# Two unsplit products instead of five in the first pair of four stages, and X's parts in another order

## The chip, the cores and the metric

The kernel runs on one core of a Trainium2 chip. The metric is the device time of one execution in microseconds (us). The engines are TensorE (PE in the profile; PEld is its weight load), VectorE (DVE), ScalarE (ACT), GpSimd (POOL) and SyncE (SP), which issues most of the DMAs.

## The reference

One layer of a streaming encoder, for 1024 prompt frames and 32 sample frames (T = 1056 tokens, D_MODEL = 1024, D_FF = 2816), all in float32:

```
attn_branch = o.reshape(B, T, Q_W) @ w_attn_out
lru_branch = (h * jax.nn.gelu(yg)) @ w_lru_out
x = x + (g_a * attn_branch + g_b * lru_branch) @ w_o
gate, up = jnp.split(rms_norm(x, ffn_norm) @ w_gate_up, 2, axis=-1)
x = x + (jax.nn.silu(gate) * up) @ w_down
```

Ahead of it stand the input projection, windowed attention and a gated linear recurrence. The change touches the products with `w_attn_out` and `w_down` alone.

## The kernel before

The last five matrix products run from about 728 us to the end. They are cut into seven stages (`PHASES`): W_lru_out, W_attn_out, W_o, W_gate_up, and W_down in three stages of 8, 8 and 6 tiles of its 22 input tiles (`DOWN_ROWS` = 4, 4, 3 for each half). A stage goes over *pairs*: a pair is two tiles of 128 output features for all 1056 tokens. There are 4 pairs in a stage and 22 in W_gate_up, 46 in all, numbered through.

**Seven products.** A pair computes a 2 x 2 block product (output tile x token half, with the contraction cut in two halves) with seven block products instead of eight. This needs sums of W's quarters (`w_sum`, GpSimd, four for each pair, into `wsum` and in place into `praw`) and of X's quarters (`x_sum`, VectorE, four for each stage, in place in `acc` and `spare`). X's seven parts are the same for all pairs of a stage; part 2 is X's second sum, part 5 a plain quarter. A product is done for two token quarters of 264, each with 4 chunks of 128 of the contraction (3 in the last stage), into the banks of `BANKS`: products 4, 5 and 6 add onto the banks of 0, 1 and 3 once those are copied or combined.

**Split and unsplit.** Most products are split: each operand is a high part rounded to the fast matmul format (fp32r) and a low part, its remainder, and a chunk is three matmuls (high x high, low x high, high x low of X and W). The high parts are made by ScalarE (`w_high` L1153 into `wsh`, `x_high` L1170 into `xh`), the low parts of W by GpSimd (`w_low` L549 into `wsl`), those of X by VectorE (`part_low` L1518 into `xl`). W's parts go through a ring of four slots (`SLOTS`): the high part of a split product waits until TensorE has ended the split product four before it. X's parts stay for the whole stage. A product in `FP32` is unsplit in the first pair of its stage: TensorE takes float32 operands as they are, one matmul for a chunk (two records in the trace), and waits for the raw part only. This bridges the time until X's parts are made.

**Combination.** VectorE adds the products up (`combine`): `first_sums` (L1615, L1619) after product 2, then one combination for each of products 3 to 6. In the W_down stages (`combine_added`) three adds of 528 columns (L1675) put the sums onto the rows of the residual right behind `first_sums`; in W_attn_out (`combine_gated`) gates are applied behind each product.

**Order.** Each engine's order is written out by hand. VectorE's is the loop over pairs that the change edits. `LOWS` and `HIGHS` say in which order X's parts are counted, for the waits; `x_high_after` and `w_high_after` say behind which product ScalarE makes a part; GpSimd goes product by product (`w_sum`, `w_low`). A sum of W that overwrites `wsum` waits until its last reader is done: GpSimd's own `w_low` for a split product, TensorE for an unsplit one.

Of the kernel before, what the change touches and what calls it, by code (L numbers as in the profile page):

```python
# [155 lines left out]
PLAIN_BANKS = {(0, 0): 2, (1, 1): 0, (0, 1): 4, (1, 0): 6}  # L156
FP32 = ((0, 1, 2, 3, 4, 5, 6), (2, 3, 4, 5, 6), (2, 3, 4, 5, 6), (0, 2, 3, 4, 5, 6)) + ((2, 3, 4, 5, 6),) * 3
X_FIRST = tuple(f + (f == PLAIN) for f in PHASE_FIRST[:PHASES])
BANKS = ((0, 1), (4, 5), (2, 3), (6, 7), (0, 1), (4, 5), (6, 7))
LOWS = ((0, 1, 2, 3, 4, 5, 6),) * 3 + ((1, 0, 2, 3, 4, 5, 6),) + ((0, 1, 2, 3, 4, 5, 6),) * 3  # L160
HIGHS = ((0, 1, 2, 4, 5, 3, 6), (0, 1, 4, 5, 2, 3, 6), (0, 1, 2, 5, 4, 3, 6), (1, 0, 5, 2, 3, 4, 6)) + ((0, 1, 4, 5, 2, 3, 6),) * 3
MERGED_LRU = 3 * PAIRS[LRU_OUT]
# [83 lines left out]
def x_high_after():  # L246

    at = {(0, 0): [(LRU_OUT, 2)], (0, 1): [(LRU_OUT, 4), (LRU_OUT, 5)], (0, 2): [(LRU_OUT, 3)], (0, 4): [(LRU_OUT, 6)]}
    for t in range(1, PHASES):
        f = X_FIRST[t]  # L250
        if t == GATE_UP:
            order = {(f, 0): (5, 2), (f, 1): (3,), (f, 2): (4,), (f, 4): (6,)}
        elif t == OUT:
            order = {(f - 1, 0): (0,), (f - 1, 1): (1,), (f, 0): (2, 5), (f, 1): (4, 3), (f, 4): (6,)}
        else:
            order = {(f - 1, 0): (0,), (f - 1, 1): (1,), (f - 1, 4): (4,), (f - 1, 5): (5,),
                     (f, 0): (2,), (f, 1): (3,), (f, 4): (6,)}
        for pr, ks in order.items():
            at.setdefault(pr, []).extend((t, k) for k in ks)
# [7 lines left out]
def build(nc, small_in, x_in, cs_in, w_in, kc_in, vc_in, y_out, kp_out, vp_out, ks_out, vs_out, tail_out):  # L267
# [17 lines left out]
    with ctx:  # L285
# [987 lines left out]
        def _(dve):  # L1273
# [456 lines left out]
            for p in range(N_PAIRS):  # L1730
# [16 lines left out]
                elif first:  # L1747
                    part_low(t, 2)
                elif second:
                    part_low(t, 6 if t in (ATTN_OUT, OUT) else 5)  # L1750
                combine(p, 2)
                if nxt:
                    part_low(nxt, 1)
                if first:
                    if t == LRU_OUT:
                        part_low(t, 2)
                    x_sum(t, 3)
                elif second and t not in (ATTN_OUT, OUT):
                    part_low(t, 6)
# [5 lines left out]
                combine(p, 4)  # L1765
                if first and t in (ATTN_OUT, OUT):
                    part_low(t, 4)
# [3 lines left out]
                elif nxt:  # L1771
                    x_sum(nxt, 2)
                if first:
                    part_low(t, 5 if t in (ATTN_OUT, OUT) else 4)
                combine(p, 6)
# [325 lines left out]
```

## Time and profile before

| | |
|---|---|
| median of three runs | 1692.95 us (1692.91 to 1693.06) |
| the profiled execution | 1695.31 us, its span 1693.5 us |
| TensorE busy | 1638.5 us, 97% of the span |
| VectorE busy | 1063.5 us, 63% |
| GpSimd busy | 965.3 us, 57% |
| ScalarE busy | 619.1 us, 37% |
| matmuls split (xh, xl) | 3 x 2170 records, 1859.5 us of overlapping durations |
| matmuls unsplit (acc, spare with praw, wsum) | 716 records |

Times in a timeline row are microseconds from the span's start, then the length. Matmuls overlap in the records, so the distance between starts tells the pace, not the duration of one. A bracket at the end of a row is the engine's idle time before it and what ended it.

### The profile page before, as it was taken

Reading aid. Unit: us, or ns where it says so; the run is one execution under the profiler, and the core shown is the slowest. Engines: PE = TensorE matmul, PEld = TensorE weight load, DVE = VectorE, ACT = ScalarE, POOL = GpSimd, SP = SyncE. Lnnn points to the kernel's source line nnn. Section 1 sums busy time; section 2 is a strip of 40 time slices with the busy share of each in tenths; the row PEclk is TensorE's granted clock in tenths of the full one; section 3 lists DMA queues with packets and bytes.
Section 4 is the critical chain, followed back from the end, with each engine's and each line's share of the span. In section 5 each row is a group of like instructions: output and inputs, shape, how many; then the busy total and the mean of one; then the engine's idle time right before and its main releaser. Section 6 shows DMA issues by size and latency. Waiting matters only on the chain. (4 is left out here: it accounts for less than half of the span.)

```text
span 1693.5 us, 29231 instructions
## 1 busy us (share of the span) xinstructions
PE 1638.5 (97%) x11306; PEld 1548.2 (91%) x11306; DVE 1063.5 (63%) x1640; ACT 619.1 (37%) x1303; POOL 965.3 (57%) x687
## 2 busy tenths in 40 slices
PE   7999999999999999999899899999999999999999
PEld 4899989988889898898898889999999999998998
DVE  7777774963856556677889678333333334869685
ACT  4354533233342434433334334333333333433242
POOL 4656552321312222287785716877777777786876
PEclk9999999999999999999999999999999999999999
DMA  4111112233113131345541512222243222373734
GB/s 166 50 51 62 62 56 100 67 78 113 53 56 102 56 107 64 103 155 201 178 153 51 194 62 76 101 76 76 76 159 108 76 76 76 137 263 114 257 141 147
DMA packets 72764, 182.12 MB, mean 108 GB/s; under 512 B 14704, under 2 KB 26416, under 8 KB 72000
## 3 DMA queue, kind: packets, MB, share of 16 engines
q1 hardware_dynamic: 51376, 159.13, 26.8%
q10 hardware_dynamic: 21264, 21.27, 4.2%
q8 instruction: 85, 1.39, 0.3%
q14 instruction: 39, 0.32, 0.1%
HBM read 131.36 MB, written 49.28 MB: 107 GB/s over the span
## 5 line engine op out<-in xcount | busy, mean ns | idle before, releaser
L573 PE MATMUL bank<-xh,wsh 128*128 128x264 f32 x2170 | 622.9, 287 | 22.4 <-POOL wsl L549 6.7
L573 PE MATMUL bank<-xh,wsl 128*128 128x264 f32 x2170 | 618.6, 285 | 0.0
L573 PE MATMUL bank<-xl,wsh 128*128 128x264 f32 x2170 | 618.0, 285 | 0.0
L573 PEld LDWEIGHTS bank<-xh,wsh 128*128 128x128 f32 x2170 | 410.4, 189 | 26.1 <-issue 18.1
L573 PEld LDWEIGHTS bank<-xl,wsh 128*128 128x128 f32 x2170 | 410.6, 189 | 0.3
L573 PEld LDWEIGHTS bank<-xh,wsl 128*128 128x128 f32 x2170 | 410.5, 189 | 0.0
L573 PE MATMUL bank<-acth,wh 128*128 128x352 f32 x984 | 329.3, 335 | 4.7 <-POOL actl L511 3.8
L573 PE MATMUL bank<-acth,wl 128*128 128x352 f32 x984 | 319.9, 325 | 0.0
L573 PE MATMUL bank<-actl,wh 128*128 128x352 f32 x984 | 318.6, 324 | 0.0
L499 POOL TENSOR_SCALAR wh<-wraw 128x512 fp32r<-128x512 f32 x104 | 86.0, 827 | 382.4 <-PE bank L573 371.9
L549 POOL TENSOR_TENSOR wsl<-praw,wsh 128x512 fp32r<-128x512 f32 (+1 forms) x157 | 243.8, 1553 | 84.1 <-ACT wsh L1153 83.9
L549 POOL TENSOR_TENSOR wsl<-wsum,wsh 128x512 fp32r<-128x512 f32 (+1 forms) x120 | 187.9, 1566 | 81.6 <-ACT wsh L1153 81.5
L573 PEld LDWEIGHTS bank<-acth,wh 128*128 128x128 f32 x984 | 185.3, 188 | 9.1 <-issue 5.2
L1153 ACT ACTIVATE wsh<-praw 128x512 fp32r<-128x512 f32 (+1 forms) x157 | 96.9, 621 | 255.0 <-PE bank L573 230.2
L573 PEld LDWEIGHTS bank<-actl,wh 128*128 128x128 f32 x984 | 186.0, 189 | 3.3
L573 PEld LDWEIGHTS bank<-acth,wl 128*128 128x128 f32 x984 | 185.3, 188 | 0.4
L501 POOL TENSOR_TENSOR wl<-wraw,wh 128x512 fp32r<-128x512 f32 x104 | 152.2, 1464 | 15.2 <-POOL wh L499 0.2
L1711 DVE TENSOR_TENSOR ev<-bank,ev 128x264 f32<-128x264 f32 x126 | 53.8, 431 | 158.9 <-PE bank L573 158.9
L1153 ACT ACTIVATE wsh<-wsum 128x512 fp32r<-128x512 f32 (+1 forms) x120 | 74.2, 618 | 198.7 <-POOL wsum L545 116.6
L1518 DVE TENSOR_TENSOR xl<-acc,xh 128x2112 fp32r<-128x2112 f32 (+1 forms) x47 | 129.7, 2759 | 22.7 <-ACT xh L1170 22.7
L1615 DVE SCALAR_TENSOR_TENSOR ev<-bank,ev 128x264 f32<-128x264 f32 x90 | 38.6, 429 | 136.4 <-PE bank L573 135.8
L545 POOL TENSOR_TENSOR wsum<-praw,wsum 128x512 f32<-128x512 f32 (+1 forms) x45 | 71.5, 1589 | 80.0 <-PE bank L573 80.0
(170 smaller groups left out, 2394.8 us busy)
## 6 DMA issues: line engine op xcount, KB each, us to landing
praw<-in_weights SPq DMA_DIRECT2D x34, 1024.0 KB, 4.9
wraw<-in_weights SPq DMA_DIRECT2D x52, 512.0 KB, 3.3
h_scratch<-ev SPq DMA_DIRECT2D x44, 264.0 KB, 2.1
acc<-h_scratch SPq DMA_DIRECT2D x4, 2112.0 KB, 12.3
ev<-x_scratch SPq DMA_DIRECT2D x6, 1056.0 KB, 5.0
spare<-x_scratch SPq DMA_DIRECT2D x6, 1056.0 KB, 5.1
praw<-in_weights SPq DMA_DIRECT2D x8, 768.0 KB, 4.7
ta_scratch<-tg ACTq DMA_DIRECT2D x24, 176.0 KB, 1.9
```

What stands on the lines that cost most here:

```text
L499: nc.gpsimd.tensor_scalar(wh[:, u, c], wraw[:, u, c], 1.0, 0.0, ALU.mult, ALU.add).then_inc(split_done, 1)
L501: nc.gpsimd.tensor_tensor(wl[:, u, c], wraw[:, u, c], wh[:, u, c].bitcast(f32), ALU.subtract)\
L545: nc.gpsimd.tensor_tensor(dst, a, b, op).then_inc(wsum_done, 1)
L549: nc.gpsimd.tensor_tensor(w_slot(wsl, p, r), w_part(p, r), w_slot(wsh, p, r).bitcast(f32), ALU.subtract)\
L573: return nc.tensor.matmul(*args, **kw)
L1153: f(w_slot(wsh, p, r), w_part(p, r), ACT.Copy).then_inc(whi_done, 1)
L1518: V.tensor_tensor(xl[k][:, 0:n, :], x_part(t, k), xh[k][:, 0:n, :].bitcast(f32), ALU.subtract)\
L1615: stt(u2(par, n), bank[BANKS[2][n]][:, 0:QB], scale, u2(par, n), ALU.mult, ALU.add).then_inc(u2_done, 1)
L1711: V.tensor_tensor(dst, bank[BANKS[r][n]][:, 0:QB], (u4(par, n), None, u2(par, n), u2(par, n))[r - 3], ALU.add).then_inc(done, 1)
```

## The change

In W_attn_out and the three W_down stages `FP32` holds products 3 and 6 alone, so products 2, 4 and 5 of the first pair are split too. Their X parts move ahead of part 3: `HIGHS` and `LOWS` of these stages become 0, 1, 2, 4, 5, 3, 6. ScalarE makes high 2, 4 and 5 in the last pair of the stage before (where 4 and 5 stood, with 2 ahead), and VectorE makes low 4 and low 5 before products 3 and 4 are combined. With three products more split, each of these stages has three more high and three more low parts of W.

```diff
--- before.py
+++ after.py
@@ -154,11 +154,12 @@
 PLAIN = PHASE_FIRST[GATE_UP]
 PLAIN_ORDER = ((0, 0, 0), (0, 0, 1), (0, 1, 1), (0, 1, 0), (1, 0, 1), (1, 1, 1), (1, 0, 0), (1, 1, 0))
 PLAIN_BANKS = {(0, 0): 2, (1, 1): 0, (0, 1): 4, (1, 0): 6}
-FP32 = ((0, 1, 2, 3, 4, 5, 6), (2, 3, 4, 5, 6), (2, 3, 4, 5, 6), (0, 2, 3, 4, 5, 6)) + ((2, 3, 4, 5, 6),) * 3
+FP32 = ((0, 1, 2, 3, 4, 5, 6), (3, 6), (2, 3, 4, 5, 6), (0, 2, 3, 4, 5, 6)) + ((3, 6),) * 3
 X_FIRST = tuple(f + (f == PLAIN) for f in PHASE_FIRST[:PHASES])
 BANKS = ((0, 1), (4, 5), (2, 3), (6, 7), (0, 1), (4, 5), (6, 7))
-LOWS = ((0, 1, 2, 3, 4, 5, 6),) * 3 + ((1, 0, 2, 3, 4, 5, 6),) + ((0, 1, 2, 3, 4, 5, 6),) * 3
-HIGHS = ((0, 1, 2, 4, 5, 3, 6), (0, 1, 4, 5, 2, 3, 6), (0, 1, 2, 5, 4, 3, 6), (1, 0, 5, 2, 3, 4, 6)) + ((0, 1, 4, 5, 2, 3, 6),) * 3
+LOADED_EARLY = (ATTN_OUT, DOWN, DOWN + 1, DOWN + 2)
+LOWS = ((0, 1, 2, 3, 4, 5, 6), (0, 1, 2, 4, 5, 3, 6), (0, 1, 2, 3, 4, 5, 6), (1, 0, 2, 3, 4, 5, 6)) + ((0, 1, 2, 4, 5, 3, 6),) * 3
+HIGHS = ((0, 1, 2, 4, 5, 3, 6), (0, 1, 2, 4, 5, 3, 6), (0, 1, 2, 5, 4, 3, 6), (1, 0, 5, 2, 3, 4, 6)) + ((0, 1, 2, 4, 5, 3, 6),) * 3
 MERGED_LRU = 3 * PAIRS[LRU_OUT]
 X_LOADED = {ATTN_OUT: 32, DOWN: 64, DOWN + 1: 96, DOWN + 2: 128}
 
@@ -253,8 +254,8 @@
         elif t == OUT:
             order = {(f - 1, 0): (0,), (f - 1, 1): (1,), (f, 0): (2, 5), (f, 1): (4, 3), (f, 4): (6,)}
         else:
-            order = {(f - 1, 0): (0,), (f - 1, 1): (1,), (f - 1, 4): (4,), (f - 1, 5): (5,),
-                     (f, 0): (2,), (f, 1): (3,), (f, 4): (6,)}
+            order = {(f - 1, 0): (0,), (f - 1, 1): (1,), (f - 1, 4): (2,), (f - 1, 5): (4,), (f - 1, 6): (5,),
+                     (f, 1): (3,), (f, 4): (6,)}
         for pr, ks in order.items():
             at.setdefault(pr, []).extend((t, k) for k in ks)
     return at
@@ -1746,8 +1747,10 @@
                     part_low(t, 1)
                 elif first:
                     part_low(t, 2)
+                    if t in LOADED_EARLY:
+                        part_low(t, 4)
                 elif second:
-                    part_low(t, 6 if t in (ATTN_OUT, OUT) else 5)
+                    part_low(t, 5 if t in (LRU_OUT, GATE_UP) else 6)
                 combine(p, 2)
                 if nxt:
                     part_low(nxt, 1)
@@ -1755,7 +1758,9 @@
                     if t == LRU_OUT:
                         part_low(t, 2)
                     x_sum(t, 3)
-                elif second and t not in (ATTN_OUT, OUT):
+                    if t in LOADED_EARLY:
+                        part_low(t, 5)
+                elif second and t in (LRU_OUT, GATE_UP):
                     part_low(t, 6)
                 combine(p, 3)
                 if nxt and nxt != OUT:
@@ -1763,15 +1768,15 @@
                 if first:
                     part_low(t, 3)
                 combine(p, 4)
-                if first and t in (ATTN_OUT, OUT):
+                if first and t == OUT:
                     part_low(t, 4)
                 combine(p, 5)
                 if nxt == OUT:
                     x_sum(nxt, 1)
                 elif nxt:
                     x_sum(nxt, 2)
-                if first:
-                    part_low(t, 5 if t in (ATTN_OUT, OUT) else 4)
+                if first and t not in LOADED_EARLY:
+                    part_low(t, 5 if t == OUT else 4)
                 combine(p, 6)
                 if nxt == OUT:
                     x_sum(nxt, 2)
```

The file grows by one line above the engines' code, so line L1518 of before is L1519 of after, and so on.

VectorE, first pair of the second W_down stage (pair 38), from low 2 on, before (`xl2`, `xl5` are X's low parts, L1552 X's last sum, L1687 a combination):

```order
L1518 TENSOR_TENSOR xl2<-acc,xh2 128x2112 [waits x_part_high]
L1615 SCALAR_TENSOR_TENSOR ev<-bank2,ev 128x264 [waits first_product_copied,product_done]
L1619 SCALAR_TENSOR_TENSOR ev<-bank4,ev 128x264 [waits residual_added,u2_done]
L1615 SCALAR_TENSOR_TENSOR ev<-bank3,ev 128x264 [waits first_product_copied,product_done]
L1619 SCALAR_TENSOR_TENSOR ev<-bank5,ev 128x264 [waits residual_added,u2_done]
L1675 TENSOR_TENSOR ev<-ev 128x528 [waits u4_done,rows_loaded0]
L1675 TENSOR_TENSOR ev<-ev 128x528 x2
L1552 TENSOR_TENSOR acc<-acc 128x4x528 [waits x_part_low,product_done,x_sums,hidden_loaded]
L1687 SCALAR_TENSOR_TENSOR ev<-bank6,ev 128x264 [waits residual_added,product_done]
```

and after the change:

```order
L1519 TENSOR_TENSOR xl2<-acc,xh2 128x2112 [waits x_part_high]
L1519 TENSOR_TENSOR xl4<-acc,xh4 128x2112 [waits x_part_high]
L1616 SCALAR_TENSOR_TENSOR ev<-bank2,ev 128x264 [waits first_product_copied,product_done]
L1620 SCALAR_TENSOR_TENSOR ev<-bank4,ev 128x264 [waits residual_added,u2_done]
L1616 SCALAR_TENSOR_TENSOR ev<-bank3,ev 128x264 [waits first_product_copied,product_done]
L1620 SCALAR_TENSOR_TENSOR ev<-bank5,ev 128x264 [waits residual_added,u2_done]
L1676 TENSOR_TENSOR ev<-ev 128x528 [waits u4_done,rows_loaded0]
L1676 TENSOR_TENSOR ev<-ev 128x528 x2
L1553 TENSOR_TENSOR acc<-acc 128x4x528 [waits x_part_low,x_sums,hidden_loaded]
L1519 TENSOR_TENSOR xl5<-acc,xh5 128x2112 [waits x_part_high]
L1688 SCALAR_TENSOR_TENSOR ev<-bank6,ev 128x264 [waits residual_added,product_done]
```

Low 4 has moved ahead of the first sums, low 5 ahead of the combination of product 3; before, low 4 stood four products on and low 5 in the next pair. X's last sum no longer waits for TensorE's product 2.

ScalarE, from behind product 4 of pair 37 into pair 38, before:

```order
L1153 ACTIVATE wsh0<-wsum 128x512 [waits weight_sums,product_done]
L1170 ACTIVATE xh4<-acc 128x2112 [waits product_done,hidden_loaded]
L1153 ACTIVATE wsh1<-praw1 128x512 [waits pair_weights_loaded1,product_done]
L1170 ACTIVATE xh5<-acc 128x2112 [waits product_done,hidden_loaded]
L1209 ACTIVATE ev<-bank0 128x264 [waits product_done]
L1209 ACTIVATE ev<-bank1 128x264 [waits product_done]
L1170 ACTIVATE xh2<-acc 128x2112 [waits product_done,x_sums]
```

and after (`wsh` is a high part of W, L1209 and L1210 the copy of product 0):

```order
L1171 ACTIVATE xh2<-acc 128x2112 [waits product_done,x_sums]
L1154 ACTIVATE wsh3<-wsum 128x512 [waits weight_sums,product_done]
L1171 ACTIVATE xh4<-acc 128x2112 [waits product_done,hidden_loaded]
L1154 ACTIVATE wsh0<-praw0 128x512 [waits pair_weights_loaded0,product_done]
L1171 ACTIVATE xh5<-acc 128x2112 [waits product_done,hidden_loaded]
L1210 ACTIVATE ev<-bank0 128x264 [waits product_done]
L1210 ACTIVATE ev<-bank1 128x264 [waits product_done]
L1154 ACTIVATE wsh1<-wsum 128x512 [waits weight_sums,product_done]
```

High 2, which waits for X's sums, has moved from behind the copy to the front, with the high parts of W for products 2 and 4 of pair 38 and the copy behind it.

GpSimd, pair 38 from the low part for product 1 on, before:

```order
L549 TENSOR_TENSOR wsl0<-wsum,wsh0 128x512 [waits weight_high]
L545 TENSOR_TENSOR praw0<-praw0 128x4x128 [waits weight_sums]
L545 TENSOR_TENSOR wsum<-praw0,wsum 128x512 [waits product_done]
L545 TENSOR_TENSOR wsum<-praw1 128x512 [waits pair_weights_loaded1]
L549 TENSOR_TENSOR wsl1<-praw1,wsh1 128x512 [waits weight_high]
L549 TENSOR_TENSOR wsl2<-wsum,wsh2 128x512 [waits weight_high]
L545 TENSOR_TENSOR wsum<-wsum,praw1 128x512 [waits product_done,weight_sums]
```

and after, from the same low part on:

```order
L550 TENSOR_TENSOR wsl2<-wsum,wsh2 128x512 [waits weight_high]
L546 TENSOR_TENSOR praw0<-praw0 128x4x128 [waits weight_sums]
L550 TENSOR_TENSOR wsl3<-wsum,wsh3 128x512 [waits weight_high]
L546 TENSOR_TENSOR wsum<-praw0,wsum 128x512 [waits weight_low]
L550 TENSOR_TENSOR wsl0<-praw0,wsh0 128x512 [waits weight_high]
L550 TENSOR_TENSOR wsl1<-wsum,wsh1 128x512 [waits weight_high]
L546 TENSOR_TENSOR wsum<-praw1 128x512 [waits pair_weights_loaded1]
```

Low parts of W for products 2, 4 and 5 have come in, and the sum for product 5 waits for GpSimd's own low part (`weight_low`) where it waited for TensorE (`product_done`).

## Rows read from the trace of the kernel before

**Rows 1.** The page: its span and its first part.
```profile
span 1693.5 us, 29231 instructions
...
PE 1638.5 (97%) x11306; PEld 1548.2 (91%) x11306; DVE 1063.5 (63%) x1640; ACT 619.1 (37%) x1303; POOL 965.3 (57%) x687
```

**Rows 2.** Timeline of TensorE: start, us, group, shapes, count.
```profile
1545.28 3.72 PE L573 MATMUL bank<-acc,wsum 128*128 128x264 f32 x16
1548.84 7.28 PE L573 MATMUL bank<-acc,praw 128*128 128x264 f32 x32
...
1559.52 3.72 PE L573 MATMUL bank<-acc,praw 128*128 128x264 f32 x16
```

**Rows 3.** Windows: stretch, its us, TensorE busy, clock, DMA.
```profile
1496.67:1517.12 20.45, 20.45 (x170) 1.00 0.82 307
1659.76:1675.07 15.31, 15.31 (x128) 1.00 0.39 142
```

**Rows 4.** Timeline of VectorE, second W_down stage.
```profile
1536.12 2.75 DVE L1552 TENSOR_TENSOR acc<-acc 128x2112 f32<-128x2112 f32 x1
...
1542.42 0.76 DVE L1687 SCALAR_TENSOR_TENSOR spare<-bank,spare 128x264 f32<-128x264 f32 x2
1544.84 2.36 DVE L1518 TENSOR_TENSOR xl<-acc,xh 128x2112 fp32r<-128x2112 f32 x1 [1.66 <-ACT xh L1170]
1547.26 0.43 DVE L1615 SCALAR_TENSOR_TENSOR ev<-bank,ev 128x264 f32<-128x264 f32 x1
...
1550.04 4.27 DVE L1675 TENSOR_TENSOR ev<-ev 128x528 f32<-128x528 f32 x3
1554.23 3.42 DVE L1552 TENSOR_TENSOR acc<-acc 128x2112 f32<-128x2112 f32 x1
```

**Rows 5.** Timeline of ScalarE, the same stage.
```profile
1532.28 1.96 ACT L1170 ACTIVATE xh<-acc 128x2112 fp32r<-128x2112 f32 x1
```

**Rows 6.** Timeline of GpSimd, the same stage; in brackets the idle before.
```profile
1536.62 3.40 POOL L545 TENSOR_TENSOR praw<-praw 128x512 f32<-128x512 f32 x1
1549.08 1.27 POOL L545 TENSOR_TENSOR wsum<-praw,wsum 128x512 f32<-128x512 f32 x1 [9.07 <-PE bank L573]
```

**Rows 7.** Waits of TensorE in second pairs (us, times, longest), and two timeline rows.
```profile
PE bank L573 <- DVE ev L1648: 2.2, 2, 1.5
PE bank L573 <- POOL wsl L549: 2.1, 1, 2.1
...
1581.28 0.37 PE L573 MATMUL bank<-xh,wsh 128*128 128x264 f32 x1 [0.54 <-DVE spare L1687]
...
1657.32 0.36 PE L573 MATMUL bank<-xh,wsh 128*128 128x264 f32 x1 [1.03 <-DVE spare L1687]
```

**Rows 8.** Timelines of VectorE and TensorE, first W_down stage.
```profile
1453.20 1.78 DVE L1719 TENSOR_TENSOR ev<-ev 128x528 f32<-128x528 f32 x1
...
1457.50 3.72 PE L573 MATMUL bank<-acc,wsum 128*128 128x264 f32 x16
...
1471.74 3.72 PE L573 MATMUL bank<-acc,praw 128*128 128x264 f32 x16
```

**Rows 9.** Timelines of VectorE and TensorE, third W_down stage.
```profile
1627.18 0.76 DVE L1687 SCALAR_TENSOR_TENSOR spare<-bank,spare 128x264 f32<-128x264 f32 x2
...
1640.23 2.83 PE L573 MATMUL bank<-acc,praw 128*128 128x264 f32 x12
...
1654.21 2.62 DVE L1518 TENSOR_TENSOR xl<-acc,xh 128x1584 fp32r<-128x1584 f32 x1
```

**Rows 10.** Timelines of VectorE and TensorE, W_attn_out stage.
```profile
803.83 3.72 PE L573 MATMUL bank<-acc,wsum 128*128 128x264 f32 x16
...
804.46 0.71 DVE L1654 SCALAR_TENSOR_TENSOR spare<-spare,ev 128x528 f32<-128x528 f32 x1
807.82 3.31 DVE L1518 TENSOR_TENSOR xl<-acc,xh 128x2112 fp32r<-128x2112 f32 x1 [2.65 <-ACT xh L1170]
...
818.07 3.72 PE L573 MATMUL bank<-acc,praw 128*128 128x264 f32 x16
```

## The prediction

> **What bounds the kernel now.** I read the page's busy shares first: TensorE works 97% of the span [rows 1], so the time moves only with what TensorE issues and with what makes it wait. Then I read TensorE's timeline in the stages that change. In the first pair of the second W_down stage products 2 to 6 are unsplit: product 2 is 16 records from 1545.28, product 3 begins at 1548.84, product 6 at 1559.52 [rows 2]. So one unsplit product takes 1548.84 - 1545.28 = 3.56 us, and five of them end at 1559.52 + 3.72 = 1563.24 with no gap. A pair with all seven products split takes 20.45 us, 2.92 us each; with three chunks 15.31, 2.19 each [rows 3]. An unsplit product of three chunks takes 3/4 of 3.56, 2.67 us. A split product is therefore 0.64 us (0.48) shorter, if its parts are ready. The rest of the reading is who makes them ready: VectorE's timeline beside it (all of X's sums and low parts), ScalarE's (the high parts) and GpSimd's (sums and low parts of W).
>
> **What the change removes on TensorE.** In four stages products 2, 4 and 5 of the first pair become split: 3 x 3 x 0.64 + 3 x 0.48 = 5.8 + 1.4 = 7.2 us less matmul time. That is 0.4% of the span, and would be the whole story if no part came late.
>
> **What it adds elsewhere.** Twelve more high parts of W on ScalarE and low parts on GpSimd. ScalarE has room. What matters is VectorE. X's low parts are not new, all seven were made before; but now TensorE needs low 2, 4 and 5 within the first pair, while before it took the raw part there. The order shows VectorE doing low 2, low 4, the two first sums of product 2 (four instructions), three adds of residual rows, X's last sum, and only then low 5. From the end of product 2 TensorE has product 3 (3.56) and product 4 (2.92), 6.48 us, before it wants low 5.
>
> **The chain in the second W_down stage.** VectorE ends the pair before at 1542.42 + 0.76 = 1543.18 [rows 4]. High 2 now stands one pair earlier on ScalarE and waits there for X's second sum, which ends at 1536.12 + 2.75 = 1538.87; with 1.96 us for it [rows 5] it is there by 1540.9, before VectorE is free, and high 4, another 1.96 with one short weight part between, well before low 2 ends. So VectorE goes straight on. What a low part costs depends on GpSimd. With GpSimd idle, low 2 took 2.36 us; the sum beside a busy GpSimd took 3.42, and the three adds 4.27 [rows 4]; GpSimd's own row beside VectorE took 3.40 [rows 6]. I price an X operation at 3.4 where GpSimd has work. It has: the idle of 9.07 us before its row at 1549.08, waiting for the unsplit product 2 [rows 6], is gone with that wait, and three more low parts stand there. Low 2 starts as GpSimd has only begun, so 2.36 + 0.4: 1545.9. TensorE, ready at 1545.28, loses 0.6 and ends product 2 at 1545.9 + 2.92 = 1548.8. Low 4 ends at 1549.3; the sums, 4 x 0.43, at 1551.0; the adds at 1555.3; X's last sum at 1558.7; low 5 at 1562.1. TensorE wanted it at 1548.8 + 6.48 = 1555.3: it **waits 6.8 us**. Product 5 and the unsplit product 6 follow, 2.92 + 3.56 = 6.48, and the pair ends at 1568.6 instead of 1563.24: +5.35. In the next pair TensorE had waited 0.54 us for VectorE [rows 7]; with VectorE's low parts now done earlier that wait goes. Net **+4.8**. Product 6 needs the bank that the combination behind low 5 frees (0.76 us), during product 5: nothing.
>
> **The first W_down stage**, the same way: VectorE is free at 1453.20 + 1.78 = 1454.98 [rows 8]. Low 2 to 1457.9; the low part of W for product 2 stands behind it on GpSimd and takes 1.2 more, so product 2 runs 1459.1 to 1462.0 (before, it began at 1457.50 [rows 8]). The second half of its sums ends at 1463.1, then 4.27 + 3.4 + 3.4: low 5 at 1474.2, pair end 1480.7 against 1471.74 + 3.72 = 1475.46: +5.2, less about 0.5 as above: **+4.7**.
> **The third**, with three chunks: free at 1627.18 + 0.76 = 1627.94; a low part takes 2.62 beside GpSimd [rows 9], and 3/4 of 2.36, 1.8, alone. Low 2 to 1630.0, low 4 to 1632.6, sums 1634.3, adds 1638.6, sum 1641.2, low 5 1643.8; then 2.19 + 2.67 gives 1648.7 against 1640.23 + 2.83 = 1643.06: +5.6, less the 1.03 of the next pair [rows 7]: **+4.6**.
> **W_attn_out** differs: product 2's combination has no three adds. VectorE is free at 804.46 + 0.71 = 805.17 [rows 10] with GpSimd's backlog ahead of it: low 2 at 808.5, so product 2, which began at 803.83 [rows 10], starts 4.7 later and ends at 811.4. Low 4 811.9, sums 813.6, sum 817.0, low 5 820.4 against 817.9 wanted; the end is 820.4 + 6.48 = 826.9 against 818.07 + 3.72 = 821.8, +5.1. But in its second pair TensorE had waited 2.2 us on VectorE's lag and 2.1 on a late low part of W [rows 7], which came of GpSimd waiting for the unsplit product 5. VectorE starts 2.6 us earlier than its row at 807.82 [rows 10], which had waited for high 2, and GpSimd no longer waits: -4.3. Net **+0.8**.
>
> **The sum.** 4.8 + 4.7 + 4.6 + 0.8 = +14.9 us on the profiled span of 1693.5, in which the 7.2 us saved are already counted. That execution took 1695.31 with what lies around the span; the median of the three runs is 1692.95. I add to the median: 1707.9, say **1708.0** (+0.9%).
>
> **The lock.** The rows show that a VectorE operation on two SBUF tensors grows from 2.36 to 3.4 us beside GpSimd, while its operations from PSUM stay at 0.43 [rows 4]. The Trainium skill, "SBUF — State Buffer", section "Who interferes with whom", says that the two engines share a port pair as an exclusive lock: a VectorE instruction with two SBUF inputs and a GpSimd one that reads SBUF block each other for the whole of the first. The trace agrees in kind. By that rule alone each X operation could wait for a full GpSimd one; an estimate from the page's rule, 2.36 + GpSimd's 1.27 = 3.6 us, would be 0.2 us more for each, 3 us more in all. A simple sharing of bandwidth would leave short waits shorter, so the rule speaks against this change.
>
> **Bounds of what the trace does not show.** VectorE unhindered: in a W_down stage low 5 comes 2 x 0.43 (sums of the last half) + 3 x 0.71 (as a 528-column row of [rows 10]) + 2 x 2.36 = 7.7 us after product 2's end, 1.2 after it is wanted. Then a stage gives 3 x -0.64 + 1.2 - 0.5 = -1.2. In W_attn_out low 2 is there at 807.5 and low 5 in time: +1.6 - 4.3 = -2.7. From above: each X operation with the full 3.4 and each low part of W for product 2 another 1.2 late, +1.2 a stage, and nothing regained in W_attn_out's second pair: +8.
>
> **Rivals.**
> *The parts come in time* (the other side). Wait at most 1.2 us: -2.7 - 3 x 1.2 = -6.3, or 1686.6; with no wait at all it would be -7.2, and -4.3, -0.5, -0.5 and -1.0 in the second pairs, 1679.5. A W_down stage wins when low 5 comes less than 6.48 + 1.92 + 0.5 = 8.9 us after product 2's end. For it: GpSimd leaves gaps where ScalarE is held back by its slots. Against: even unhindered VectorE is late, and it has eleven units of GpSimd work beside it.
> *Half hindered.* GpSimd idles during X's last sum and low 5, so 2.36 each: low 5 is 2.1 us earlier, +2.7 a stage; with -1 in W_attn_out, 3 x 2.7 - 0.2 = +7.9: 1701.
> *A second wait.* Putting high 2 ahead on ScalarE, where it waits for X's sum until 1538.87, holds back the W high parts and the copy of product 0 behind it; if the W parts then come late as well, or W_attn_out's second pair regains nothing: 1708 + 4 to 8, 1712 to 1716.
>
> **How the numbers follow.** The forecast 0.62; half hindered 0.15; second wait 0.11; parts in time 0.12. The range 1697 to 1713 holds the forecast and its neighbours and leaves out the last case and the far end of the second wait. Within 0.2% (3.4 us) is about what a measurement of this kernel cannot tell from no change. Faster 0.12, same 0.05, slower 0.83.
>
> **What the changed profile would show.** Right: TensorE idle of 5 to 7 us before product 5 of the first pair in each W_down stage, released by VectorE's low part; idle near 4 us before product 2 in W_attn_out; GpSimd without its idle of 9 us; VectorE's X operations at 3.4 beside it; second pairs at 20.45 us. Wrong: X operations at 2.4, or a gap under 2 us, or the wait released by GpSimd's low part of W. The prediction fails first if VectorE meets less of GpSimd than I assume.

## The result, and the profile after

The changed kernel takes **1718.15 us** (median of 4 runs, 1716.07 to 1719.61) against 1693.01 us of the kernel before beside it (4 runs, 1692.91 to 1695.46): a ratio of 1.0142, with a 95% interval of 1.0129 to 1.0155, or +25.1 us. It is slower, as forecast, but by 10 us more than the 1708.0 of the forecast and outside its range. The profiled execution took 1719.34 us.

The page of the changed kernel, its span and its first part, as in [rows 1]:

```profile
span 1717.2 us, 29443 instructions
...
PE 1643.1 (96%) x11396; PEld 1558.0 (91%) x11396; DVE 1066.5 (62%) x1640; ACT 625.6 (36%) x1315; POOL 992.8 (58%) x699
```

TensorE's busy time should have fallen by 7.2 us. It rose by 4.6, from 1638.5 [rows 1]: its work takes longer than the durations of before say. The windows of TensorE show where. They are the first pairs of the four stages (W_attn_out, then the three W_down stages), and then three pieces of the second W_down stage's first pair: the stop, the records behind it, and what follows. Columns: stretch, its us, busy, granted clock, DMA share, GB/s.

```profile
797.87:827.74 29.87, 23.76 (x152) 0.94 0.29 109
1451.83:1486.37 34.54, 25.65 (x154) 0.85 0.22 80
1549.30:1581.33 32.03, 24.57 (x154) 0.89 0.19 68
1642.65:1667.92 25.27, 19.50 (x116) 0.86 0.24 86
...
1572.00:1577.00 5.00, 4.53 (x20) 0.50 0.02 5
1577.00:1581.00 4.00, 4.00 (x22) 0.97 0.00 0
```

The same four first pairs of the kernel before had a clock of 1.00 in all four:

```profile
797.09:821.81 24.72, 23.90 (x130) 1.00 0.35 132
1451.11:1475.48 24.37, 23.93 (x130) 1.00 0.30 112
1539.16:1563.25 24.09, 23.89 (x130) 1.00 0.25 90
1625.33:1643.08 17.75, 17.75 (x98) 1.00 0.34 123
```

TensorE's timeline of the changed kernel, second W_down stage: product 3 (unsplit), the first records of product 5 behind the stop, then product 6.

```profile
1559.08 3.72 PE L574 MATMUL bank<-acc,praw 128*128 128x264 f32 x16
...
1572.47 0.56 PE L574 MATMUL bank<-xh,wsh 128*128 128x264 f32 x1 [6.75 <-issue]
1572.83 0.42 PE L574 MATMUL bank<-xl,wsh 128*128 128x264 f32 x1
1573.05 0.42 PE L574 MATMUL bank<-xh,wsl 128*128 128x264 f32 x1
...
1577.59 3.72 PE L574 MATMUL bank<-acc,praw 128*128 128x264 f32 x16
```

The bracket names no engine (`issue`). That the stop is the wait for low 5 is read from the times: low 5 ends at 1572.37 (below) and the first record of product 5 starts 0.1 us behind it, and the distance is the same in experiment 3 (1557.42 and 1557.52), where low 5 ends 4 us sooner in the pair. Behind this stop of 6.75 us the records of product 5 follow one another 0.22 us apart; elsewhere the same records are 0.12 apart, a split product taking 2.92 us in 24 of them. The stretch 1572 to 1577 has a granted clock of 0.50, the level of 1.2 GHz instead of 2.4. Product 5 takes 1577.6 - 1572.4 = 5.2 us and not 2.92.

VectorE's timeline, the same stage (what answers to [rows 4]), and GpSimd's (to [rows 6]):

```profile
1561.07 4.63 DVE L1676 TENSOR_TENSOR ev<-ev 128x528 f32<-128x528 f32 x3
1565.62 3.41 DVE L1553 TENSOR_TENSOR acc<-acc 128x2112 f32<-128x2112 f32 x1
1568.96 3.41 DVE L1519 TENSOR_TENSOR xl<-acc,xh 128x2112 fp32r<-128x2112 f32 x1
```

```profile
1560.45 1.27 POOL L550 TENSOR_TENSOR wsl<-wsum,wsh 128x512 fp32r<-128x512 f32 x1
1561.68 1.74 POOL L546 TENSOR_TENSOR wsum<-praw 128x512 f32<-128x512 f32 x1
1563.38 1.76 POOL L550 TENSOR_TENSOR wsl<-praw,wsh 128x512 fp32r<-128x512 f32 x1
1565.10 1.72 POOL L550 TENSOR_TENSOR wsl<-wsum,wsh 128x512 fp32r<-128x512 f32 x1
1566.78 3.37 POOL L546 TENSOR_TENSOR wsum<-wsum,praw 128x512 f32<-128x512 f32 x1
```

VectorE works without a gap to the end of low 5 at 1572.4. X's last sum and low 5 take 3.41 each (low 2 and low 4 took 6.13 together), and GpSimd's 9.07 us of idle are gone.

From TensorE's timelines, each pair's time read from the end of the last record of the pair before to the end of its own last record (us):

| stage | first pair before, after | second pair before, after | change | forecast |
|---|---|---|---|---|
| W_attn_out (its third pair -1.0) | 24.72, 29.87 | 25.50, 21.11 | -0.3 | +0.8 |
| W_down 1 | 24.37, 34.54 | 21.19, 20.45 | +9.4 | +4.7 |
| W_down 2 | 24.09, 32.03 | 21.18, 20.43 | +7.2 | +4.8 |
| W_down 3 (its third pair +0.1) | 17.75, 25.27 | 16.68, 15.42 | +6.4 | +4.6 |

The sum is +22.7; the spans differ by 1717.2 - 1693.5 = 23.7, so 1 us lies outside these pairs. Of it 0.8 lies ahead of W_attn_out's first pair (797.87 - 797.09); its cause wasn't looked for.

### The profile page after: what moved, and what is told of

Read it like the earlier page. It is cut to its first block, busy times and chain, and to the rows that moved or that the text cites. A ratio compares the mean times of both kernels' runs of the same rounds, so it can differ in the third digit from the quotient of the medians.

```text
span 1717.2 us, 29443 instructions
## 1 busy us (share of the span) xinstructions
PE 1643.1 (96%) x11396; PEld 1558.0 (91%) x11396; DVE 1066.5 (62%) x1640; ACT 625.6 (36%) x1315; POOL 992.8 (58%) x699
## 4 chain that ended last, share of the span: by engine, by line
PE 63%; POOL 5%; DVE 5%; issue 4%; DMA 3%; ACT 1%; SPq 0%; DVEq 0%; ACTq 0%; POOLq 0%
PE bank L574 62%; POOL wsl L550 3%; POOL wsum L546 2%; PE bank L746 1%; DMA praw<-in_weights 1%; DVE xl L1519 1%; DMA ev<-ta_scratch 1%; DVE ev L1655 1%; DVE qstd L1439 1%; DMA mb_scratch<-ev 1%; DMA ev<-in_x 0%; DVE ev L1649 0%; DVE pr L1490 0%; POOL praw L546 0%; DVE acc L1662 0%
## 5 line engine op out<-in xcount | busy, mean ns | idle before, releaser
L574 PE MATMUL bank<-xh,wsh 128*128 128x264 f32 x2260 | 654.2, 289 | 42.3 <-issue 24.9
L574 PE MATMUL bank<-xh,wsl 128*128 128x264 f32 x2260 | 648.7, 287 | 0.0
L574 PE MATMUL bank<-xl,wsh 128*128 128x264 f32 x2260 | 648.0, 287 | 0.0
L574 PEld LDWEIGHTS bank<-xh,wsh 128*128 128x128 f32 x2260 | 432.2, 191 | 46.6 <-issue 38.9
L574 PEld LDWEIGHTS bank<-xl,wsh 128*128 128x128 f32 x2260 | 432.4, 191 | 0.4
L574 PEld LDWEIGHTS bank<-xh,wsl 128*128 128x128 f32 x2260 | 432.0, 191 | 0.0
L550 POOL TENSOR_TENSOR wsl<-wsum,wsh 128x512 fp32r<-128x512 f32 (+1 forms) x128 | 203.7, 1591 | 89.6 <-ACT wsh L1154 89.5
L1154 ACT ACTIVATE wsh<-wsum 128x512 fp32r<-128x512 f32 (+1 forms) x128 | 79.0, 617 | 180.6 <-POOL wsum L546 100.6
L1519 DVE TENSOR_TENSOR xl<-acc,xh 128x2112 fp32r<-128x2112 f32 (+1 forms) x47 | 132.7, 2830 | 16.9 <-ACT xh L1171 16.9
L546 POOL TENSOR_TENSOR wsum<-praw,wsum 128x512 f32<-128x512 f32 (+1 forms) x45 | 77.2, 1717 | 52.5 <-PE bank L574 52.2
```

What stands on the lines that cost most here:

```text
L546: nc.gpsimd.tensor_tensor(dst, a, b, op).then_inc(wsum_done, 1)
L550: nc.gpsimd.tensor_tensor(w_slot(wsl, p, r), w_part(p, r), w_slot(wsh, p, r).bitcast(f32), ALU.subtract)\
L574: return nc.tensor.matmul(*args, **kw)
L1154: f(w_slot(wsh, p, r), w_part(p, r), ACT.Copy).then_inc(whi_done, 1)
L1519: V.tensor_tensor(xl[k][:, 0:n, :], x_part(t, k), xh[k][:, 0:n, :].bitcast(f32), ALU.subtract)\
```

## The experiments

The theory: the stops are as forecast, made by VectorE's chain beside GpSimd, and the missing 10 us are TensorE's clock behind them. The rivals are named with each run. "Parts" of a product's time below are wait, its 2.92 (3.56) us at full pace, and the rest. A bracket gives a stop about 0.1 us longer than these parts do (6.75 and 6.65 for the stop above).

A ratio is to the kernel before, measured on the same occasion. Its medians were 1695.08 us beside experiments 1, 3, 4 and 5, 1694.93 beside 2, 6, 7 and 10, and 1694.46 beside 8, 9 and 11, where it had been 1693.01 beside the changed kernel. So a difference from the changed kernel's 1718.15 is good to some 2 us only.

**1. The stops filled with matmuls.** The kernel after, with matmuls on constants in front of the waits, as many as the waits are long; the waits themselves stay.

```diff
+KEEP = {(ATTN_OUT, 2): 10, (DOWN, 2): 4, (DOWN, 5): 14, (DOWN + 1, 5): 14, (DOWN + 2, 5): 12}
...
+def keep_busy(t, r, b):
+    for _ in range(KEEP.get((t, r), 0)):
+        mm(b[:, QB:QB + 248], small1[:, 0:P], small1[:, 0:248], start=True, stop=True, skip_group_check=True)
...
+                    if p == X_FIRST[t] and r == 2:
+                        keep_busy(t, r, bank[BANKS[1][0]])
...
+                            if p == X_FIRST[t] and r == 4 and n == 1 and j == len(parts) - 1:
+                                keep_busy(t, 5, bank[BANKS[4][1]])
```

> The changed kernel, with matmuls on constants that nothing reads ahead of the waits in first pairs: 10 and 4 ahead of product 2 in W_attn_out and the first W_down stage, 14, 14 and 12 ahead of product 5 in the three W_down stages, each some 0.41 us, so shorter in all than the waits they fill (4.8, 1.8, 6.5, 6.6 and 5.5 us). They move no wait's end. Theory A (the clock: after TensorE has stood for the wait on X's low part the granted clock is 0.5 for 3.4 to 6.8 us, and products behind the wait run at that pace): the clock stays at 1.0 in these stages, the product behind each wait takes its wait plus 2.92 us, pair 38 takes 29.5 instead of 32.0 us, and the whole falls by 9 to 11 us, to about 1708. Theory B (these products are slow for another reason, such as the restart or GpSimd's and VectorE's load): nothing falls, 1718.

Measured 1708.15 us (1707.58 to 1709.44), ratio 1.0076 (1.0060 to 1.0093): 10.0 us less than the changed kernel, with more work on TensorE. Windows of the first pairs of W_down 1 and 2, and TensorE's timeline around product 5 of the second:

```profile
1449.69:1480.19 30.50, 29.87 (x190) 1.00 0.24 90
1543.13:1573.03 29.90, 28.31 (x182) 1.00 0.20 74
```

```profile
1559.27 6.02 PE L575 MATMUL bank<-small 128*128 128x248 f32 x28
...
1566.31 0.36 PE L575 MATMUL bank<-xh,wsh 128*128 128x264 f32 x1 [0.89 <-issue]
1566.51 0.29 PE L575 MATMUL bank<-xl,wsh 128*128 128x264 f32 x1
1566.63 0.28 PE L575 MATMUL bank<-xh,wsl 128*128 128x264 f32 x1
```

VectorE's chain is untouched (low 5 3.42 us), and what the constants take with the wait left over, 5.86 + 0.78 = 6.6 us, is the old stop; but the clock is 1.00 and the records are 0.12 apart. So the stop and the slow products behind it are two costs. From the first W_down pair to the last matmul this trace has 253.4 us and the changed kernel's 262.2: the clock there was worth 8.9 us. W_attn_out's pairs gained nothing (its first pair kept its length, as low 5 then came late by 1.6 us instead of 0.3), and the other 2.1 us by which the two profiled spans differ more lie ahead of 797 us, where the two kernels are the same. These matmuls disturb sums standing in the bank that they are written to (the last section).

**2. The same without the start flag** on the constants' matmuls, which leaves those sums alone.

```diff
-        mm(b[:, QB:QB + 248], small1[:, 0:P], small1[:, 0:248], start=True, stop=True, skip_group_check=True)
+        mm(b[:, QB:QB + 248], small1[:, 0:P], small1[:, 0:248], start=False, stop=True, skip_group_check=True)
```

> The first experiment again (the changed kernel with matmuls on constants in front of the waits), with one difference: they add onto what lies in their columns instead of starting anew. Theory A (those matmuls take the same time either way, and it is the clock that they save): 1708, as before, 10 us below the changed kernel. Theory B (the time of the first experiment hung on that flag): another time.

Measured 1710.03 (1709.18 to 1710.9), ratio 1.0089 (1.0071 to 1.0106), clock 1.0 in the four stages: the first finding doesn't hang on the disturbed sums.

**3. GpSimd held back.** The kernel after; in each W_down stage GpSimd begins the second pair's work only when low 5 is made.

```diff
+                    if r == 0 and t >= DOWN and p == X_FIRST[t] + 1:
+                        pool.wait_ge(xlo_done, nth_low(t, 5))
```

> The changed kernel, but in the three W_down stages GpSimd begins the weights of the second pair only once X's low 5 is done. Theory A (the wait at product 5 is VectorE's chain, stretched by GpSimd beside it): the three adds take some 2.2 instead of 4.6 us, X's last sum and low 5 some 2.4 instead of 3.4 each, low 5 is 4 us earlier, TensorE waits 2.7 instead of 6.6 us; 12 us less in all, 1706, and if so short a stop leaves the clock at 1.0 about 7 more, 1699. Weights of the second pair were 10 to 17 us early and stay in time. Theory B (the chain's length is VectorE's own and waits for TensorE and DMAs set it): durations unchanged, 1718.

Measured 1699.9 (1695.91 to 1704.28, 5 runs), ratio 1.0032 (1.0013 to 1.0051), 18 us less than the changed kernel. Timelines of VectorE, GpSimd and TensorE, second W_down stage:

```profile
1550.43 2.45 DVE L1678 TENSOR_TENSOR ev<-ev 128x528 f32<-128x528 f32 x3
1552.81 2.34 DVE L1555 TENSOR_TENSOR acc<-acc 128x2112 f32<-128x2112 f32 x1
1555.08 2.34 DVE L1521 TENSOR_TENSOR xl<-acc,xh 128x2112 fp32r<-128x2112 f32 x1
```

```profile
1557.50 1.29 POOL L546 TENSOR_TENSOR wsum<-praw 128x512 f32<-128x512 f32 x1 [6.42 <-DVE xl L1521]
```

```profile
1557.52 0.37 PE L576 MATMUL bank<-xh,wsh 128*128 128x264 f32 x1 [2.42 <-issue]
```

With GpSimd idle the adds take 2.45 instead of 4.63 us, the sum and low 5 2.34 instead of 3.41: 4.3 us of the 6.65 us stop came of running beside GpSimd. Of the stop 2.3 us stay, more than the 1.2 of the prediction's lower bound, since the adds take 2.45 and not 3 x 0.71 and low 4 still ends late. The clock stayed at 1.00 behind that stop.

**4. Low 5 first.** The kernel after; VectorE makes low 5 ahead of the three adds and X's last sum.

```diff
                     first_sums(p, scale, i)
+                    if t >= DOWN and p == X_FIRST[t]:
+                        part_low(t, 5)
...
-                    if t in LOADED_EARLY:
+                    if t == ATTN_OUT:
                         part_low(t, 5)
```

> The changed kernel, but in the three W_down stages VectorE makes low 5 right behind the first sums, ahead of the three adds and X's last sum. Theory A (place in VectorE's order): low 5 is in time for product 5, no stop there. The adds (4.6), the last sum (3.4) and the combination of product 3 (0.8) then end some 13.4 us after product 2 where product 6 wants them 9.4 after it, so the wait moves to product 6 and is 4 us instead of 6.6; product 6 is unsplit. 2.6 us a stage less, 1710, and with a shorter stop perhaps 3 to 7 less through the clock, 1703 to 1710. Theory B (any place in this pair costs the same, since VectorE's total work is what is late): 1716 to 1718.

Measured 1707.72 (1707.41 to 1711.61), ratio 1.0080 (1.0063 to 1.0096). The stop moved one product on, to X's sum for product 6 and its bank, and the clock fell behind it all the same (0.94, 0.94, 0.92 in the three first pairs). TensorE's timeline, second stage:

```profile
1567.08 5.44 PE L574 MATMUL bank<-acc,praw 128*128 128x264 f32 x16 [4.24 <-DVE ev L1690]
```

16 records take 5.44 us here and 3.72 at full pace [rows 2]. The order was worth some 10 us of the 25, more than theory B allowed; but with either order VectorE's work in the pair is done late, and TensorE stops for it.

**5. Both, 3 and 4 together** (GpSimd released after low 5, which now stands ahead of the adds).

> Both of the two edits together: low 5 right behind the first sums, and GpSimd begins the second pair's weights only after it. GpSimd is then released while the adds and the last sum still run. Theory A: low 5 in time; the adds and the last sum still meet GpSimd in part, so a wait of 2 to 4 us at product 6 stays and the clock holds; 1698 to 1706. If GpSimd stayed away during all of it the wait would be gone and the time below that of before, 1686 to 1690. Theory B (nothing but VectorE's total work counts): 1712 to 1718.

Measured 1705.35 (1701.34 to 1706.99), ratio 1.0062 (1.0045 to 1.0079): within what was expected, and yet above 3 alone (from the first W_down pair to the last matmul its trace has 244.7 us, that of 3 has 242.7). The adds and X's sum now run beside GpSimd again, and product 6 takes 5.57, 6.97 and 5.84 us with its wait. The clock stayed at 1.00 behind these three stops.

**6. W_attn_out alone.** The tables of the change for W_attn_out; the W_down stages as before.

```diff
-FP32 = ((0, 1, 2, 3, 4, 5, 6), (3, 6), (2, 3, 4, 5, 6), (0, 2, 3, 4, 5, 6)) + ((3, 6),) * 3
+FP32 = ((0, 1, 2, 3, 4, 5, 6), (3, 6), (2, 3, 4, 5, 6), (0, 2, 3, 4, 5, 6)) + ((2, 3, 4, 5, 6),) * 3
-LOADED_EARLY = (ATTN_OUT, DOWN, DOWN + 1, DOWN + 2)
+LOADED_EARLY = (ATTN_OUT,)
...
```

> The change in W_attn_out alone; the three W_down stages as before. Theory A (all the loss is in W_down, W_attn_out's first pair loses what its second pair regains): within 2 us of before in the same call, clock loss of one product included. Theory B (W_attn_out takes a share of the loss, as its 4.8 us stop and its half clock suggest when the first pair is looked at alone): 4 to 6 us above before.

Measured 1696.86 (1692.41 to 1700.4, 10 runs) against 1694.93 for the kernel before beside it (1689.37 to 1698.06, 29 runs), ratio 1.0016 (1.0002 to 1.0029). Its pairs are those of the changed kernel, and so is the window:

```profile
796.47:826.34 29.87, 23.97 (x152) 0.94 0.29 109
```

By the ratio W_attn_out costs 2.7 us, with an interval of 0.3 to 4.9, so the times alone don't exclude theory B. In the trace its first three pairs together take 0.3 us less than before, as in the changed kernel; where the rest of the difference comes from isn't known. The +23.0 of the table are W_down's.

**7. 3 with the rest of its stops filled** (matmuls on constants without the start flag: 10, 4, 2, 4, 4 of them).

> The kernel in which GpSimd waits for X's low 5 in the W_down stages, with matmuls on constants ahead of the waits as in the first experiment, fewer of them (10 and 4 ahead of product 2 in W_attn_out and the first W_down stage, 2, 4 and 4 ahead of product 5). Their columns of a bank are read by nobody, and they add onto what lies there instead of starting anew. Theory A (that kernel's runs of 1696 to 1704 spread because its stops are just long enough to lose the clock in some): 1693 to 1696, and the runs within 1.5 us of each other. Theory B (the spread has another cause, such as DMA): the spread stays.

Measured 1697.69 (1694.25 to 1700.53, 10 runs), ratio 1.0014 (1.0002 to 1.0025). That it is nearly level with the kernel before was expected; that the runs would then lie close together was not borne out. They spread over 6 us, and the kernel before over 8.7 beside them. The spread isn't explained.

**8. A stop alone, long.** The kernel **before**, with no split product added: TensorE waits ahead of product 5 of the W_down first pairs for VectorE's combination of product 4 (`c11_done`). Nothing else is changed.

```diff
+                    if t >= DOWN and p == X_FIRST[t] and r == 5:
+                        pe.wait_ge(c11_done, 2 * nth(p) + 2)
```

> The kernel before, with nothing but a stop of TensorE ahead of product 5 in the first pair of each W_down stage: it waits there for VectorE's combination of product 4, which by the trace of before ends 5.3, 5.3 and 5.0 us after product 5 would start. 15.6 us of stops, less 2.0 of waits in second pairs that go. Theory A (a stop of this length costs the clock too, and products 5 and 6 behind it, 7.1 us of unsplit matmuls, run at half pace for some 6.8 us): 13.6 + 3 x 3.4 = 24 us above before, with a granted clock of 0.5 behind each stop. Theory B (a stop costs its length): 14 us above before.

Measured 1718.63 (1716.95 to 1720.13), ratio 1.0144 (1.0130 to 1.0159), +24 us. Timeline of TensorE and window of the first pair, second W_down stage:

```profile
1570.49 5.75 PE L573 MATMUL bank<-acc,wsum 128*128 128x264 f32 x16 [5.21 <-DVE ev L1689]
1576.07 3.72 PE L573 MATMUL bank<-acc,praw 128*128 128x264 f32 x16
```

```profile
1548.34:1579.81 31.47, 26.08 (x130) 0.89 0.19 69
```

The three products 5 take 11.31, 10.96 and 9.51 us, 22.0 above 3.56, 3.56 and 2.67. Of that 15.5 are the stops (5.37, 5.21 and 4.96 in the brackets) and 6.5 are products run at the lower clock, 1.9 to 2.4 us behind each stop, with about 0.3 for each that isn't the clock. The second pairs add 1.9 in all, where 2.0 less was expected: product 6 there takes 4.3 us, since it waits for the combination of product 3, and that stands behind three adds that took 5.03 us instead of 4.40. So theory A's total came out by luck: its clock term was 3.7 us too large and its second pairs 3.9 too small. What is shown is that a stop by itself costs this kernel its length and some 2 us more.

**9. A stop alone, short.** The same with the combination of product 3 (`c22_done`).

```diff
-                        pe.wait_ge(c11_done, 2 * nth(p) + 2)
+                        pe.wait_ge(c22_done, 2 * nth(p) + 2)
```

> As the long stop, but TensorE waits for the combination of product 3, which ends 2.4, 2.4 and 2.7 us after product 5 would start: 7.5 us of stops, less 2.0. Theory A (so short a stop leaves the clock at 1.0, as in the kernel where GpSimd waits): 5 to 6 us above before. Theory B (any stop there costs the clock): 5.5 + 3 x 3.4 = 16 us above before.

Measured 1707.67 (1706.81 to 1709.2), ratio 1.0081 (1.0067 to 1.0096), +13.2 us, between what the two theories gave. Timeline and windows of TensorE: the product behind the stop in stage 2, three us of it, the first pair of stage 2, that of stage 3.

```profile
1563.75 5.52 PE L573 MATMUL bank<-acc,wsum 128*128 128x264 f32 x16 [2.26 <-DVE ev L1689]
```

```profile
1564.00:1567.00 3.00, 3.00 (x8) 0.52 0.00 0
1544.54:1572.84 28.30, 25.86 (x130) 0.94 0.21 77
1635.56:1656.14 20.58, 18.02 (x98) 1.00 0.29 106
```

Behind 2.26 us the clock fell in stages 1 and 2, and the product took 1.9 us more than its stop and its 3.56 us; behind 2.56 us in stage 3 the clock stayed and only 0.3 us came on top, and it stayed behind 2.42 us in experiment 3 too. The second pairs add 1.9 us again. So the length of the stop doesn't decide alone. What else does is open.

**10. Two products split.** From the experiments: products 2 and 4 split, 5 left unsplit in W_down, so that low 5 is nobody's next input; GpSimd waits for X's last sum before the second pair; W_attn_out as before.

```diff
-FP32 = ((0, 1, 2, 3, 4, 5, 6), (3, 6), (2, 3, 4, 5, 6), (0, 2, 3, 4, 5, 6)) + ((3, 6),) * 3
+FP32 = ((0, 1, 2, 3, 4, 5, 6), (2, 3, 4, 5, 6), (2, 3, 4, 5, 6), (0, 2, 3, 4, 5, 6)) + ((3, 5, 6),) * 3
-LOWS = ((0, 1, 2, 3, 4, 5, 6), (0, 1, 2, 4, 5, 3, 6), (0, 1, 2, 3, 4, 5, 6), (1, 0, 2, 3, 4, 5, 6)) + ((0, 1, 2, 4, 5, 3, 6),) * 3
+LOWS = ((0, 1, 2, 3, 4, 5, 6),) * 3 + ((1, 0, 2, 3, 4, 5, 6),) + ((0, 1, 2, 4, 3, 5, 6),) * 3
...
+                    if r == 0 and t >= DOWN and p == X_FIRST[t] + 1:
+                        pool.wait_ge(xsum_done, 4 * t + 4)
```

> The kernel before, but in the three W_down stages products 2 and 4 of the first pair are split and product 5 stays unsplit (low 5 behind the combination of product 5, in time for the second pair), high 2 ahead as in the change, and GpSimd begins the second pair's weights once X's last sum is done. W_attn_out as before. Theory A (what must not stand on the path is low 5 behind the adds and the last sum): TensorE gains 2 x 0.64 us a stage, loses 1.8, 0.4 and 0.1 at product 2, regains 0.5 to 1.0 in second pairs: 3 to 4 us below before. Theory B (low 4 ahead of the sums delays the adds and the sum enough to stop product 6): 0 to 5 us above before.

Measured 1694.4 (1689.89 to 1698.05, 12 runs), ratio 0.9995 (0.9984 to 1.0007): the same as before. The stages are 26.78, 23.57 and 17.24 us in their first pairs: two gained 0.5 each, the first lost 2.4, as the low part of W for product 2 was 1.81 late and the clock fell behind that (0.94 in the pair).

**11. The same, that part earlier.** GpSimd makes the low part of W for product 2 ahead of the sum for product 3, and begins the second pair after the three adds. The edit against experiment 10:

```diff
-                        pool.wait_ge(xsum_done, 4 * t + 4)
+                        pool.wait_ge(v_done, 3 * (PAIRS[OUT] + p - PHASE_FIRST[DOWN]))
+                    swap = t >= DOWN and p == X_FIRST[t] and r == 2
+                    if swap:
+                        w_low(p, r)
...
-                    if not in_fp32(p, r):
+                    if not in_fp32(p, r) and not swap:
```

> The kernel with products 2 and 4 split in the three W_down stages, with two edits on GpSimd: in their first pairs it makes the low part of W for product 2 ahead of the sum for product 3, and in their second pairs it begins once the three adds of residual rows are done, some 2 us earlier than before. Theory A (what was left of waits there is GpSimd's order: product 2 of the first W_down stage stood 1.8 us for its low part of W, the second pair of the third stage 0.9 us): product 2 there waits 0.7 us, the stages take 44.2, 44.0 and 32.7 us against 45.6, 45.3 and 34.4 of before, 4 us below before in all. Theory B (VectorE takes back what GpSimd gains, since they meet again during X's last sum): equal to before or above.

Measured **1690.72** (1688.92 to 1695.33, 12 runs) against 1694.46 (17 runs), ratio 0.9984 (0.9974 to 0.9994): faster than both kernels, and than the one before by 3.7 us by the medians and 2.7 by the ratio (1.0 to 4.4). Windows of its three first pairs:

```profile
1448.73:1472.85 24.12, 22.87 (x146) 1.00 0.30 113
1535.79:1559.36 23.57, 22.84 (x146) 1.00 0.26 93
1620.70:1637.94 17.24, 17.05 (x110) 1.00 0.35 126
```

The first and second pairs of the three stages take 121.99 us together instead of 125.26: the first pairs gain 1.3, the second pairs 2.0. That is 0.7 less than theory A's 4.

## Why the prediction was right in direction and wrong in size

**The step that failed** is the end of each first pair: "Product 5 and the unsplit product 6 follow, 2.92 + 3.56 = 6.48", and the same in the other stages, priced at the durations of a TensorE that had not stopped. Behind the stops it ran at a granted clock of 0.50. The parts of product 5 are 6.47 + 2.92 + 1.98 in W_down 1, 6.65 + 2.92 + 2.47 in W_down 2 and 5.47 + 2.19 + 2.2 in W_down 3, where product 6 took another 0.8 (3.51 for 2.67); products 2 of W_attn_out and W_down 1 lost 1.7 and 1.8. That is 11 us in all, of which about 0.3 per stop isn't the clock (experiment 1 has it too: wait, 2.92, 0.33). Experiment 1 takes it away and lands on 1708.15, experiment 2 on 1710.03, where 1708.0 was forecast; experiment 8 makes it with a stop alone. The forecast was +14.9 and +25.1 came: 8.9 of these 10.2 us stand in the W_down pairs, W_attn_out came out 1.1 better than forecast, 1.0 lies in the span outside the pairs of the table, and 1.4 is what the medians differ by more than the two profiled spans. So that experiment 1 lands within 0.2 us of the forecast is partly luck. No rival of the prediction named the clock, though the kernel before had its granted clock printed beside each window that it rests on [rows 3].

**What held.** *The chain of VectorE and the stop.* Low 5 was forecast 6.8 us late in W_down 2 and was 6.65 late. By the prediction's steps it would be 1474.2 - (1462.0 + 6.48) = 5.7 late in W_down 1, and was 6.47, since the adds took 5.23 us there and not 4.27. In W_down 3 they make 1643.8 - (1630.0 + 2.19 + 4.86) = 6.8, and it was 5.47: the adds took 3.58 us beside GpSimd's shorter instructions of three chunks. So W_down 3's forecast of +4.6 was too long in the wait and too short in the clock, and +6.4 came out. *X operations at 3.4 beside GpSimd* were 3.41 for X's last sum and low 5, and 2.34 with GpSimd idle (experiment 3): shown. The rule of the Trainium skill, "SBUF — State Buffer", section "Who interferes with whom", that the port pair of the two engines is an exclusive lock, fits in kind (a block for the whole instruction the page states of VectorE's 2-port modes; of two SBUF inputs it says that they contend): three adds of 528 columns grew most, from 2.45 to 4.63 and 5.23. The 3.6 us estimated from it alone for an X operation was too much; the measured row of before, 3.42 [rows 4], was the better price. *GpSimd's idle gone, second pairs at 20.45*: 20.45 and 20.43, so 0.7 regained in each of two and 1.3 in the third, a little more than the 0.5, 0.5 and 1.0 forecast.

**W_attn_out.** Product 2 was forecast to start 4.7 later; its wait was 4.83. Its first pair lost 5.15 (5.1 forecast), but in other parts: before product 5 0.25 instead of 2.5, and 1.7 for the clock behind product 2, time in which VectorE caught up; X's last sum took 2.52 and not 3.4. The second pair gave back 4.4 (4.3). The right total here is partly two errors that cancel. In the bound for a VectorE unhindered the prediction's +1.6 should be 807.5 - 803.83 - 1.92 = +1.8, which changes nothing.

**The rivals.** *The parts come in time* is refuted by the stops, and experiment 3 shows that even without GpSimd they would not. *Half hindered* is refuted: the sum and low 5 ran at 3.41 each. *A second wait* named a true place: high 2 waited 6.51 us on ScalarE for X's sum. But W's high parts behind it held up no product in W_down 2. Its price of 4 to 8 us happens to come near the measured gap by another mechanism, which doesn't confirm it.

**The range** was built only from how late the parts might be. With a term of some 2 us for each of five stops the forecast would have been 1718; that this meets the measured time is chance too, since W_attn_out's stop didn't lengthen its pair.

## What to carry to other kernels

Price a stop of TensorE as its length and what the products behind it lose at the lower clock, here 1.7 to 3.0 us behind each stop of 2 to 7 us, where the clock fell; a row with 1.00 in the clock column gives a duration only for a TensorE that was kept fed. A split that saves 0.64 us of matmul time needs all its parts in time: count the work of the engine that makes them between the product before and this one, at the price that it has beside a busy neighbour (3.41 us and not 2.34 here). Where one part can't be there, leave that product unsplit and take the others: experiment 11, which needed a new order on GpSimd too (experiment 10 without it gained nothing), gained 3.7 us (1.0 to 4.4 by the ratio) where the whole change lost 25.

## What the runs showed of the hardware that was not expected

- Stops of like length don't cost alike. Behind 2.26 us the granted clock of the next 3 us was 0.52 (experiment 9, stage 2), behind 2.42 us (experiment 3) and 2.56 us (experiment 9, stage 3) the pair had 1.00. Ahead of product 2 of W_down 1 TensorE stood for 1.86 to 1.88 us in the changed kernel and in experiments 3, 4, 5 and 10; the clock fell in all of them but 4. And two stops of 3.17 us ahead of the same unsplit product 6, in experiment 4 (W_down 1) and in experiment 5 (W_down 2), went differently:

```profile
1475.31 5.25 PE L574 MATMUL bank<-acc,praw 128*128 128x264 f32 x16 [3.17 <-DVE ev L1690]
```

```profile
1565.28 3.80 PE L576 MATMUL bank<-acc,praw 128*128 128x264 f32 x16 [3.17 <-DVE ev L1692]
```

The 16 records took 5.25 us in the one and 3.80 in the other; what makes the difference is open.

- In experiment 1 the matmuls on constants carried the start flag and wrote columns of a bank that no one reads, while a product was being summed in other columns of it; the sums were changed (the output y by 0.15, relative). Without the flag (experiment 2) they weren't. Which of the products was hit wasn't looked into; by the kernel both places lie in a bank onto which a later matmul still adds (product 5 onto bank 4, the last matmul of product 4 onto bank 1). The Trainium skill, "PSUM — Partial Sum Buffer", section "The four PSUM rules", has the rule: a first matmul makes the next ones overwrite in the whole bank, whichever part of it it writes. The two runs agree with it.
- One kernel's times spread more on some occasions than on others: the kernel before over 2.6 us beside the changed one, over 8.7 us beside experiments 2, 6, 7 and 10. Only with 10 and more runs can the differences of 2 to 4 us in experiments 6, 7, 10 and 11 be read.
